# Half of the first tile's expert selection and the gate vectors, moved into the two gated merges

## The reference, cut to what matters

```
# merge of the four mixers
gates = jax.nn.sigmoid(gl.reshape(b, s, N_BRANCH, D_MODEL) + lp["b_gate"])
merged = gates[:, :, 0] * y_f + gates[:, :, 1] * y_c + gates[:, :, 2] * y_a + gates[:, :, 3] * y_w
return merged @ lp["w_out"], ctx_tensors
...
# experts, 128 tokens at a time
q = (hc @ w_q).reshape(PEER_CHUNK, PEER_HEADS, 2, PEER_HALF)
sc = jnp.einsum("chpd,pkd->chpk", q, subkeys).astype(jnp.float32)
s_half, i_half = lax.top_k(sc, PEER_TOPK)
cand = s_half[:, :, 0, :, None] + s_half[:, :, 1, None, :]
cand_idx = i_half[:, :, 0, :, None] * N_KEYS + i_half[:, :, 1, None, :]
top_s, top_pos = lax.top_k(cand.reshape(...), PEER_TOPK)
eidx = jnp.take_along_axis(cand_idx.reshape(...), top_pos, axis=-1)
gate = jax.nn.softmax(top_s, axis=-1)
u = u_tab[eidx]; v = v_tab[eidx]
act = jax.nn.gelu(jnp.einsum("chkd,cd->chk", u, hc).astype(jnp.float32))
return jnp.einsum("chk,chkd->cd", (gate * act).astype(v.dtype), v)
...
# trunk layer
x = x + g1 * mix
x = x + g2 * peer_ffn(h, ...)
```

## Time and profile before

| | us |
|---|---|
| median of 3 runs | 5704.44 (5702.1 to 5712.31) |
| the profiled execution | 5690.06 |
| its span, first to last instruction | 5688.3 |
| PE busy | 4484.2 (79%) |
| DVE busy | 3691.5 (65%) |
| POOL busy | 1597.8 (28%) |
| ACT busy | 890.1 (16%) |
| share of the chain that ended last | PE 39%, DMA 34%, DVE 17%, issue 3%, ACT 3% |
| mean granted TensorE clock | 0.902 |

### The profile page before, as it was taken

The page is one execution under the profiler, slowest core; times in us unless marked ns, Lnnn a source line. Parts: engine busy times, 40 slices in busy tenths (PEclk is TensorE's granted clock), DMA queues, the critical chain, the costliest instruction groups (busy, mean ns, idle before and its releaser), DMA issues.

```text
span 5688.3 us, 47082 instructions
## 1 busy us (share of the span) xinstructions
PE 4484.2 (79%) x14736; PEld 2602.6 (46%) x14736; DVE 3691.5 (65%) x8127; ACT 890.1 (16%) x2536; POOL 1597.8 (28%) x1310
## 2 busy tenths in 40 slices
PE   4999997799788666666669999967897976766675
PEld 3766686344443222222248666854444432222222
DVE  0565415788677888876517554166886878888765
ACT  1023301111111111111110232011111111111111
POOL 0000000343334454445300000003442334444552
PEclk8999998899899888888879999989997998888887
DMA  6100042799988999999851001428998899999996
GB/s 248 60 30 1 18 156 100 304 379 371 372 349 348 422 421 421 421 420 421 332 212 52 30 1 45 144 110 330 384 372 348 353 363 421 421 421 421 420 421 283
DMA packets 226377, 1585.28 MB, mean 279 GB/s; under 512 B 26064, under 2 KB 28368, under 8 KB 46672
## 3 DMA queue, kind: packets, MB, share of 16 engines
q0 software_dynamic: 184320, 1342.26, 58.2%
q1 hardware_dynamic: 41808, 240.02, 11.2%
HBM read 1579.03 MB, written 3.15 MB: 278 GB/s over the span
## 4 chain that ended last, share of the span: by engine, by line
PE 39%; DMA 34%; DVE 17%; issue 3%; ACT 3%; DVEq 2%; POOL 1%; SPq 0%; POOLq 0%; ACTq 0%
DMA B<-tables,R 17%; PE ps L476 8%; DMA A<-tables,R 7%; PE ps L486 5%; PE ps L596 5%; DMA H<-tables,R 4%; DVE A L1426 4%; DVE B L1394 3%; DMA B<-ws 3%; PE ps L581 2%; PE ps L493 2%; PE ps L506 2%; PE ps L701 2%; DVE A L1394 2%; PE ps L688 2%
## 5 line engine op out<-in xcount | busy, mean ns | idle before, releaser
L476 PE MATMUL ps<-B,A 128*128 128x512 f32 x2048 | 1166.8, 716 | 544.8 <-ACT A L868 544.3
L444 POOL DMA_INDIRECT B<-tables,R x716 | 875.8, 1223 | 1837.0 <-PE ps L476 787.3
L1394 DVE SCALAR_TENSOR_TENSOR B<-B,M 128x1024 f32<-128x1024 f32 x716 | 867.5, 1225 | 295.8 <-DMA B<-tables,R 268.0
L476 PEld LDWEIGHTS ps<-B,A 128*128 128x128 f32 x2048 | 441.2, 225 | 1191.5 <-ACT A L868 672.2
L476 PE MATMUL ps<-A 128*128 128x512 f32 x992 | 536.5, 676 | 159.7 <-ACT A L868 159.6
L486 PE MATMUL ps<-H,B 128*128 128x384 f32 (+1 forms) x2048 | 593.1, 444 | 66.4 <-DMA B<-ws 44.9
L444 POOL DMA_INDIRECT A<-tables,R x356 | 441.9, 1241 | 583.7 <-PE ps L476 367.7
L486 PEld LDWEIGHTS ps<-H,B 128*128 128x128 f32 x2048 | 398.9, 195 | 258.2 <-DMA B<-ws 49.9
L1394 DVE SCALAR_TENSOR_TENSOR A<-A,M 128x1024 f32<-128x1024 f32 x356 | 433.6, 1224 | 123.7 <-DMA A<-tables,R 111.6
L862 ACT ACTIVATE T<-T 128x2 f32<-128x2 f32 (+1 forms) x448 | 92.5, 206 | 2357.9 <-DVEq L1396 2346.4
L476 PEld LDWEIGHTS ps<-A 128*128 128x128 f32 x992 | 211.4, 221 | 455.6 <-issue 237.1
(11 more groups left out here) (206 smaller groups left out, 5067.5 us busy)
## 6 DMA issues: line engine op xcount, KB each, us to landing
B<-ws SPq DMA_DIRECT2D x120, 1024.0 KB, 5.1
B<-ws SPq DMA_DIRECT2D x128, 768.0 KB, 4.7
B<-tables,R POOLq DMA_INDIRECT x716, 22.2
A<-tables,R POOLq DMA_INDIRECT x356
R<-tabs SPq DMA_DIRECT2D x2, 2176.0 KB, 8.7
H<-tables,R POOLq DMA_INDIRECT x192, 20.2
x<-xin SPq DMA_DIRECT2D x1, 2560.0 KB, 9.0
y<-M SPq DMA_DIRECT2D x1, 2560.0 KB, 7.9
```

Of the source, the lines that this page charges most:

```text
L444: pool.indirect_dma_start(out=ring[s], out_offset=None, in_=tables[:, :], in_offset=bass.IndirectOffsetOnAxis(ap=EI[:, n:n + 1], axis=0),) ...
L476: mm = pe.matmul(ps[:, bk + c, :], diag[PE_AT[n] % DIAGS], v_row[:, c * 512:(c + 1) * 512], start=(n % SLOTS == 0), stop=(PE_AT[n] + 1 == ...
L1394: v.scalar_tensor_tensor(out=u_row, in0=u_row, scalar=1.0, in1=h2[:, g.tile, :], op0=ALU.mult, op1=ALU.mult, accum_out=dots[:, o:o + 1])
```

## The change

The gate vectors' rounds become functions of a round (`gate_diagonals` on DVE, `gate_rows` on PE and ACT). Round i now stands in the merge of chunk 0, in its steps 4i + 1 (PE, ACT) and 4i - 2 (DVE), and uses PSUM banks 4 and 5. In the score stage DVE copies the scores of all eight heads, and selects heads 0 to 3 only. The selections of heads 4 to 7, and those of tile 1 behind them, then stand two parts to a step in steps 0 to 15 of chunk 1's merge (one between the two groups, one behind), and one part to a step from step 16 on, as before. The expert work of tile 0 begins when four heads are selected; its gates are divided in two halves, the second at slot 64. Place 5 of the ring, which lies over the scores, is added at slot 40, so the ring has five places until then.

```
-RING = 6
+RING = 5
...
+OPENS = [(0, SLOTS // 2)] + [(0,)] * (TILES - 1)
...
-LATER = {132: (6,), 236: (7, 8, 9, 10, 11), 352: (12,), 400: (13,), 528: (14,)}
+LATER = {40: (5,), 132: (6,), 236: (7, 8, 9, 10, 11), 352: (12,), 400: (13,), 528: (14,)}
...
# PE
-                for i in range(8):
+                def gate_rows(i):
                     pe.wait_ge(rw_dg.sem, rw_dg.at(l, i + 1))
                     pe.wait_ge(rw_ev.sem, rw_ev.at(l, i - 1))
-                    pe.matmul(ps[:, i % 2, :], onesD, T[:, 0:512], start=True, stop=True).then_inc(rw_ps.sem, 1)
-                pe.wait_ge(rw_ev.sem, rw_ev.at(l, 8))
+                    pe.matmul(ps[:, 4 + i % 2, :], onesD, T[:, 0:512], start=True, stop=True).then_inc(rw_ps.sem, 1)
                 pe.wait_ge(ot_ev.sem, ot_ev.at(l, TILES))
                 pe.wait_ge(ln_o.sem, ln_o.at(l, 1))
                 for s in range(N_MG):
                     mix_gates(l, 0, s)
                     mix_branch(l, 0, s)
+                    if s % 4 == 1:
+                        gate_rows(s // 4)
...
# ACT, experts(q)
-                if g.place == 0:
-                    act.wait_ge(ei_ok.sem, ei_ok.at(l, (g.tile + 1) * PH))
-                    gates = GT[:, g.tile * SLOTS:(g.tile + 1) * SLOTS]
+                if g.place in OPENS[g.tile]:
+                    heads = PH // len(OPENS[g.tile])
+                    act.wait_ge(ei_ok.sem, ei_ok.at(l, g.tile * PH + g.place // TOPK + heads))
+                    gates = GT[:, g.slots[0]:g.slots[0] + heads * TOPK]
                     act.activation(gates, gates, ACT.Exp).then_inc(g_exp.sem, 1)
...
# DVE
+                gate_diagonals(0)
                 for s in range(N_MG):
                     mix(0, s)
+                    if s % 4 == 2 and s < N_MG - 4:
+                        gate_diagonals(s // 4 + 1)
+                v.wait_ge(rw_ev.sem, rw_ev.at(l, 8))
...
                     score_copy(0, 2 * h)
                     score_copy(0, 2 * h + 1)
                     v.drain()
-                    for i in range(4):
-                        select(0, h * 4 + i)
+                    if h < PH // 2:
+                        for i in range(4):
+                            select(0, h * 4 + i)
                 for s in range(N_MG):
                     if s:
                         mix(1, s - 1)
                     experts(s * MG_STEP)
+                    if s < UNITS:
+                        select(*divmod(2 * PH + 2 * s, 4 * PH))
                     experts(s * MG_STEP + 1)
-                    select(1, s)
+                    select(*divmod(2 * PH + (2 * s + 1 if s < UNITS else UNITS + s), 4 * PH))
```

More of the change, by code:

```diff
@@ L325, in program @@
         got = [sig(f"got{b}", 16 * TURNS[b]) for b in range(HOMES)]
-        g_exp = sig("g_exp", TILES)
+        g_exp = sig("g_exp", TILES + 1)
         u_done = sig("u_done", N_GROUPS)
@@ L1004, in _, with gate_rows @@
                     attention(t + 1, t)
-                for i in range(8):
+                def gate_rows(i):
                     act.wait_ge(rw_ps.sem, rw_ps.at(l, i + 1))
-                    act.activation(grow[:, i // 4, (i // 2) % 2, (i % 2) * 512:(i % 2 + 1) * 512], ps[:, i % 2, :],
+                    act.activation(grow[:, i // 4, (i // 2) % 2, (i % 2) * 512:(i % 2 + 1) * 512], ps[:, 4 + i % 2, :],
                                    ACT.Copy, scale=float(CONV) * (0.5 if i < 4 else 1.0)).then_inc(rw_ev.sem, 1)
@@ L1263, in _, with gate_diagonals @@
                     attention(t + 1, t)
-                for i in range(8):
+                def gate_diagonals(i):
                     if i:
@@ L1396, in products, with gates @@
                     v.drain().then_inc(u_done.sem, 1)
-                def gates(t):
-                    v.wait_ge(g_exp.sem, g_exp.at(l, t + 1))
-                    e3 = GT[:, t * SLOTS:(t + 1) * SLOTS].rearrange("p (h k) -> p h k", h=PH)
-                    v.tensor_reduce(out=s2[:, 0:PH], in_=e3, axis=AX.X, op=ALU.add)
+                def gates(g):
+                    heads = PH // len(OPENS[g.tile])
+                    v.wait_ge(g_exp.sem, g_exp.at(l, 2 * g.place // SLOTS + 1 if g.tile == 0 else g.tile + 2))
+                    e3 = GT[:, g.slots[0]:g.slots[0] + heads * TOPK].rearrange("p (h k) -> p h k", h=heads)
+                    total, inverse = s2[:, 0:heads], s2[:, PH:PH + heads]
+                    v.tensor_reduce(out=total, in_=e3, axis=AX.X, op=ALU.add)
                     v.drain()
-                    v.reciprocal(s2[:, PH:2 * PH], s2[:, 0:PH])
+                    v.reciprocal(inverse, total)
                     v.drain()
-                    v.tensor_tensor(out=e3, in0=e3, in1=s2[:, PH:2 * PH].unsqueeze(2).broadcast_to([P, PH, TOPK]), op=ALU.mult)
+                    v.tensor_tensor(out=e3, in0=e3, in1=inverse.unsqueeze(2).broadcast_to([P, heads, TOPK]), op=ALU.mult)
                     v.drain()
@@ L1450, in experts @@
                         sums(q - 1)
-                    if g.place == 0:
-                        gates(g.tile)
+                    if g.place in OPENS[g.tile]:
+                        gates(g)
                     weights(q)
+                gate_diagonals(0)
                 for s in range(N_MG):
                     mix(0, s)
+                    if s % 4 == 2 and s < N_MG - 4:
+                        gate_diagonals(s // 4 + 1)
+                v.wait_ge(rw_ev.sem, rw_ev.at(l, 8))
                 for i in range(len(CHUNKS[0])):
```

## The result

The changed kernel takes 5668.27 us at the median (5662.34 to 5676.44, four runs) against 5708.38 us (5702.1 to 5716.31, four runs) for the kernel before: a ratio of 0.993, 95% interval 0.9911 to 0.9949. The profiled execution took 5669.35 us with a span of 5667.6; before, those were 5690.06 and 5688.3. So the two profiled executions stand 20.7 us apart, the two medians 40. That difference between the differences is what has to be explained. Among the runs of the experiments one of e3_fill (8633.18 us) and one of e6_tail (5902.86 us) were in a slow state and are left out of the medians, which with them would be 5692.12 and 5663.68.

A forecast was written before the change was run, and what follows sets the result against it. Four limits in turn: PE in chunk 0's merge, the gate-vector chain ahead of it, DVE in the score stage, then chunk 1's merge. Per layer 6.8 + 25 - 10.0 - 13.0 - 1.0 = 7.8 us, two layers 15.6: 5689 us, range 5673 to 5720.

The forecast's parts named there:

- the gate vectors' term: Chunk 0's merge starts 13.8 us earlier and pays 7.0 us for the eight moved matmuls: 6.8 us gained a layer.
- the 14 us: Median of the runs shown above the profiled kernel's 5690.06 us; the forecast change was taken from the median, 5704.4.
- The score stage: Chunk 1's merge starts near 984 instead of 997.54, its next block's load near 994: 25 us gained a layer.
- Two parts a step: Chunk 1's merge: extra parts free in steps 0 to 3; steps 10 to 15 take 14.6 us, costing 10.0 a layer.
- the full price: Rival: parts in chunk 1's merge cost 2.65 us each, first step at lower clock; 15.6 us steps, 5716 us, chance 0.12.
- the least case: Chunk 1's merge without DVE's waits for rows: a step of 11.8 us, with one more part 14.5.
- Five places: Steps 4 to 9 of chunk 1's merge, ring one place short: 15.1 us a step, costing 13.0 a layer.
- the divided gates: Gates in two halves: three more small DVE operations and one more ACT exponential, costing 1.0 us a layer.
- The ring at 17.5 us a step: Rival: steps 4 to 9 of chunk 1's merge wait for landings of 11.41 us; 5718 us, chance 0.20.
- the slow fetches: Rival: POOL's fetches in the merge slow to 1.96 us, 1.02 more a loop step; 5713 us, chance 0.05.
- The case in which everything hides: Rival: everything in the kernel hides as well as it can; 5679 us, chance 0.15.
- the good end: All good ends of the terms together, 12.6 us a layer, giving 5679 us for the whole kernel.

The follow-up runs named there:

- e3_fill: Kernel before with one idle matmul (384 columns) behind each of the eight gate matmuls, gate vectors left in place: 5691.77 us, ratio 0.998.
- e6_tail: Changed kernel with three idle matmuls in each of the last two rounds of the last tile's attention: 5663.06 us, ratio 0.9929 to the kernel before.
- the front: Kernel before, unedited, in the profiled execution that the prediction was read from: 5690.06 us profiled, 5708.38 us at the median of its runs.
- c0_before: Kernel before once more, no edit, as a control: 5706.71 us, ratio 1.0011; its profiled execution took 5719.43 us.
- e2_select_only: Changed kernel with the gate vectors put back ahead of the merge; selection, ring and expert start stay changed: 5690.58 us, ratio 0.998 to the kernel before.
- e7_before_tail: Kernel before with three idle matmuls in each of the last two rounds of the last tile's attention, nothing else: 5686.42 us, ratio 0.9968.

## Why the prediction was right or wrong

**What failed: the size of the gate vectors' term.** The prediction took 13.8 us from the last copy to the first merge matmul, subtracted 7.0, and left 6.8 a layer. That holds for an execution in which the clock stays up: with idle matmuls in both kernels, attention to query shrinks from 503.4 and 505.2 us to 496.2 and 497.6, by 7.2 and 7.6, and the merge of chunk 0 takes 174.0 us up to the first output projection against 167.2, near the 7.0 that was forecast. The second layer of the front's profile and of the changed kernel's, in which the clock did not fall either, shows the same: 500.2 against 493.3, 6.9 us. But for most executions of the kernel before it does not hold. The rounds and the first merge matmuls then run at 1.2 GHz, and moving the rounds also saves that; the prediction put this at nothing. The gates alone were worth 30.6 us by the medians: 13.6 by the forecast's own working and 17.3 from the clock by the two runs with idle matmuls make 30.9, well within what the intervals allow.

**Why most executions.** Of the four profiled executions with the rounds in their old place and no idle matmuls ahead of them (the front's, c0_before, e2_select_only, e3_fill) the clock fell in three, in both layers. And the 13 runs of the kernel before beside e7_before_tail have a mean granted clock of 0.8972, the eight of e7_before_tail 0.9014. The difference, 0.0042 of some 5700 us, is 24 us of clock; the two falls of c0_before (31.5 and 31 us at 0.51) lost 31. If nothing else differs between the two kernels, that is an estimate of about three falls in four possible ones.

**Where it could have been seen.** The prediction wrote that the median of the runs was 14 us above the profiled execution, and took the change from the median. That treats the 14 us as a constant that belongs to no stage. It was a sign that this execution lacked something that the others had: the profile was one in which the clock did not fall. The sum in the profile's own terms was 5674.5 us; the two profiled executions of the changed kernel took 5669.35 and 5667.25. In that comparison the forecast is off by 5 to 7 us; the rest of the miss is the 14 us that did not stay.

**The score stage: right, in part by luck.** The prediction gave 25 us a layer. From the first query matmul to the sigmoid of step 4 it was 183.5 and 186.5 us in the profile of the front and 186.2 and 185.8 in the repeated one, 185.5 in the mean; in the changed kernel's two profiles it was 162.2, 159.6, 159.2 and 162.1, 160.8 in the mean: 24.7 less. The mechanism was right as well. Counted from the first query matmul (896.33, before 903.17), the merge started after 79.3 us where 80.8 were forecast (984) and 94.4 stood before; it ran its first gates in 7.09 us instead of 5.4, and the next block's load began after 90.7 us (987.01) where 90.8 were forecast (994) and 116.0 stood before (1019.21). Two small errors cancelled. The first sigmoid came 29.4 us earlier in the first layer (982.72 against 1012.10), as was said, but that is luck: the query came 6.8 us earlier, and of this 4.2 had arisen ahead of the first transpose of attention (402.6 to 398.4), which the change does not touch. The gate vectors gave only 2.7 us in this layer of these two executions, since the clock fell at the end of attention in the changed kernel's and not in the other.

**Two parts a step: right.** 14.73 us in steps 10 to 15, for 14.6 forecast; the full price of 15.6 did not come. DVE's waits for rows went to nearly nothing, as the least case assumed.

**Five places: the loop was right, its price here was not.** Steps 4 to 9 took 14.77 us (15.1 forecast), and that is no more than the steps with six places took. The two bounds, DVE's work and the ring, are not added: the longer one sets the step. The prediction priced the ring with landings out of a chain that had picked the late ones; in the changed kernel, from 1050 to 1235 us, the median landing was 7.8 us and the longest 10.2. With one part a step the same five places cost about a microsecond a step. In all, steps 4 to 15 cost 19.7 us a layer more than before (176.4 against 156.7, four layers each), not the 23 forecast; so the selection brought some 4 to 5 us a layer and not 1. (The forecast's 1.0 us for the divided gates is within these measures; no run shows it alone.) Over all kernels of the table the same appears: query to step 31 is 535.2 us in the mean of the ten layers with the old selections, and 531.3 in the eight with the change's. Twice the missing 3 to 4 us, the 17.3 from the clock and the 15.6 forecast add up to the 40 measured, as far as the noise lets one say.

**The rivals.** The ring at 17.5 us a step did not come, the full price neither, and the slow fetches neither (0.94 us at the median). The case in which everything hides was nearest by its direction, but it ended at 5679, since it too stood on the median. None of the cases had a mechanism by which the kernel could gain more than 25 us: the range's low end went only 6 us past the good end.

**What stays open.** Why the clock falls in one execution and not in another is not settled. In the two executions of the kernel before, PE was busy for 13.29 and 13.30 of the last 15 us of attention, and in one of them the clock stood at 1.00, in the other it fell. Of the nine profiled executions without idle matmuls at the end of attention the clock fell there in eight in the first layer and in four in the second; of the three with them in none. The Trainium skill, TensorE: Matmul & The Clock Gate, section "What's actually happening", says that the chip watches PE's activity in a window that is not tied to the program's start; that would make executions of one program differ, but no run here can show it. The scatter that remains in the changed kernel, some 17 us, was not looked into; in e7_before_tail, where the clock does not fall at this place, the fastest run (5675.92 us) has the highest mean clock, 0.904, and the slowest (5695.77) the lowest, 0.899, so other stretches may differ in the same way.

## What to carry to other kernels

When the profiled execution lies below the median of the runs, find the stage in which they differ before a gap is carried over as a constant: read the granted clock stage by stage, and ask of every sparse stretch of PE what it costs at the lower clock. A chain of single matmuls with a wait in front of each, behind a thin end of a stage, is better laced into dense work; where it can't be moved, a few idle matmuls ahead of it are worth trying, and they tell at the same time whether the clock is the cause. Extra work for one engine belongs where the step is held by a load of fixed length: eight parts were free in steps that waited for weights, and cost 1.2 us each in steps that did not.

## What the runs showed of the hardware

Once the clock had fallen, a chain with a gap of 0.78 us in each round of 2.86 us ran at the lower level to its end (22.6 us of gate rounds at 0.50, PE busy for 17.09 of 23 us). Entered at the upper level, with idle matmuls ahead of it, the same chain with gaps of the same length stayed there (1.00, PE busy for 9.22 of 15 us), and without them too in the execution that the prediction was read from (1.00, 8.82 of 15 us). With an idle matmul in the gap the clock was back from the second round on; in the changed kernel's merge, without gaps, it was back some 6 us behind the first matmul, some 10 us after it fell. So the same instructions have two lasting courses in these traces, 15.1 and 22.6 us, and the level at which the chain is entered goes with the course. Idle matmuls just ahead of it kept the upper level in both layers of the one profile taken; without them either level occurred (1.00 and 0.50 in two executions of one program).
